# Higher gathered rows of two tiles summed by TensorE through a diagonal of gates, and the last but one block's rows copied ahead of the last weights' rests

## What is computed

```python
gates = jnp.einsum('tk,tke->te', top_w, jax.nn.one_hot(expert_id, N_EXPERTS))
gates = (gates * g_w[:, None]).astype(t.dtype)
for e in range(N_EXPERTS):
    he = jax.nn.silu(t @ w_gate[e]) * (t @ w_up[e])
    y = y + gates[:, e:e + 1] * (he @ w_down[e])
```

## Time and profile before

| | |
|---|---|
| time of 3 runs, us | 1502.73, 1507.63, 1510.17 (median 1507.63) |
| the profiled execution, us | 1509.55, of which the profiled span is 1507.7 |
| busy: PE (TensorE) / DVE (VectorE) / ACT (ScalarE) / POOL (GpSimd) | 95% / 76% / 59% / 40% |
| chain that ended last, by engine | PE 46%, DVE 25%, DMA 15%, issue 7%, ACT 5% |
| DVE sums L375 | 24 (12 a layer), median 1280 ns |
| products L2196 | 32 records (16 a layer), 592 to 1222 ns |

### The profile page before, as it was taken

The page is one execution under the profiler, slowest core; times in us unless marked ns, Lnnn a source line. Parts: engine busy times, 40 slices in busy tenths (PEclk is TensorE's granted clock), DMA queues, the critical chain, the costliest instruction groups (busy, mean ns, idle before and its releaser), DMA issues.

```text
span 1507.7 us, 20546 instructions
## 1 busy us (share of the span) xinstructions
PE 1431.0 (95%) x6830; PEld 1052.0 (70%) x6830; DVE 1152.7 (76%) x1658; ACT 887.7 (59%) x1300; POOL 595.7 (40%) x288
## 2 busy tenths in 40 slices
PE   7999999999999999999799999999989899999995
PEld 4678566567577888877556865665766788887773
DVE  5696887334489999999757958873335899999996
ACT  5733344643558878888485522348345488887880
POOL 2333364060005665554542425521400066655544
PEclk9999999999999999999899999999998899999998
DMA  6333601312149999999651421105041599999995
GB/s 228 95 84 70 222 10 47 140 59 98 70 162 340 399 399 399 398 399 399 216 185 42 112 81 71 57 1 198 1 167 42 183 362 398 398 398 398 398 388 181
DMA packets 151485, 312.75 MB, mean 207 GB/s; under 512 B 33158, under 2 KB 46380, under 8 KB 151228
## 3 DMA queue, kind: packets, MB, share of 16 engines
q1 hardware_dynamic: 140300, 271.39, 49.8%
q0 software_dynamic: 6624, 24.12, 4.3%
q10 hardware_dynamic: 4496, 16.40, 2.7%
HBM read 287.76 MB, written 29.50 MB: 210 GB/s over the span
## 4 chain that ended last, share of the span: by engine, by line
PE 46%; DVE 25%; DMA 15%; issue 7%; ACT 5%; POOL 1%; DVEq 1%; POOLq 0%; SPq 0%; ACTq 0%
PE ps L710 13%; DMA arena<-in_w_down 11%; DVE rest_w_down L1436 8%; PE ps L728 7%; PE ps L1518 4%; DVE rest_w_up L1436 4%; PE ps L1540 3%; DVE rest_w_gate L1436 2%; DVE xg_rest L1449 2%; PE ps L817 2%; PE ps L1636 2%; ACT head_w_down L1431 2%; PE ps L731 2%; DMA arena<-in_w_gate 1%; PE ps L850 1%
## 5 line engine op out<-in xcount | busy, mean ns | idle before, releaser
L2112 POOL TENSOR_TENSOR rest_w_down<-arena,head_w_down 128x2048 fp32r<-128x2048 f32 x30 | 193.4, 6448 | 189.4 <-ACT head_w_down L1431 189.4
L1436 DVE TENSOR_TENSOR rest_w_down<-arena,head_w_down 128x2048 fp32r<-128x2048 f32 x30 | 153.5, 5116 | 12.0 <-ACT head_w_down L1431 11.9
L1436 DVE TENSOR_TENSOR rest_w_gate<-arena,head_w_gate 128x2048 fp32r<-128x2048 f32 x64 | 145.8, 2279 | 0.1
L1436 DVE TENSOR_TENSOR rest_w_up<-arena,head_w_up 128x2048 fp32r<-128x2048 f32 x64 | 143.5, 2281 | 0.1
L1431 ACT ACTIVATE head_w_down<-arena 128x2048 fp32r<-128x2048 f32 x60 | 115.2, 1926 | 39.1 <-DMA arena<-in_w_down 38.9
L1431 ACT ACTIVATE head_w_gate<-arena 128x2048 fp32r<-128x2048 f32 x60 | 114.4, 1919 | 36.1 <-DMA arena<-in_w_gate 35.5
L1431 ACT ACTIVATE head_w_up<-arena 128x2048 fp32r<-128x2048 f32 x64 | 122.0, 1940 | 10.5 <-DMA arena<-in_w_up 10.4
L1420 PE MATMUL ps<-head_w_gate,xg_head 128*128 128x512 f32 x256 | 104.8, 409 | 2.5 <-DVE xg_rest L1449 1.9
L728 PE MATMUL ps<-hT,arena 128*128 128x512 f32 x224 | 104.3, 602 | 2.6 <-ACT arena L951 2.6
L1410 PE MATMUL ps<-head_w_down,he_head 128*128 128x512 f32 x240 | 99.2, 413 | 5.8 <-DVE rest_w_down L1436 2.9
L1422 PE MATMUL ps<-head_w_gate,xg_rest 128*128 128x512 f32 x256 | 101.0, 395 | 0.0
(11 more groups left out here) (381 smaller groups left out, 3519.2 us busy)
## 6 DMA issues: line engine op xcount, KB each, us to landing
arena<-in_w_gate SPq DMA_DIRECT2D x64, 1024.0 KB, 9.9
arena<-in_w_up SPq DMA_DIRECT2D x64, 1024.0 KB, 11.5
arena<-in_w_down SPq DMA_DIRECT2D x64, 1024.0 KB, 10.7
arena<-in_w_in SPq DMA_DIRECT2D x10, 1536.0 KB, 6.7
yrows<-yb ACTq DMA_DIRECT2D x30, 512.0 KB, 6.2
arena<-in_w_in SPq DMA_DIRECT2D x4, 2048.0 KB, 8.7
x<-in_x SPq DMA_DIRECT2D x8, 512.0 KB, 13.9
arena<-in_w_in SPq DMA_DIRECT2D x16, 256.0 KB, 4.9
```

Source lines behind the costliest of these rows:

```text
L1436: nc.vector.tensor_tensor(wl[q][:, c, :], raw[q][:, c, :], wh[q][:, c, :].bitcast(F32), ALU.subtract).then_inc(s_split[q], 1)
L2112: nc.gpsimd.tensor_tensor(wl[2][:, c, :], raw[2][:, c, :], wh[2][:, c, :].bitcast(F32), ALU.subtract)\
```

## The change

It makes six edits. The two scalars of `hot_rows` now hold the gate too, so that LAST comes out of TensorE already multiplied, and its sum is a plain addition of PSUM to x. A new tensor `gate_diag` holds, for tiles 2 and 3, the identity times `early`, made by two instructions on VectorE ahead of `gated(2)`. For tiles 2 and 3 TensorE adds the HIGH rows onto the LAST rows in the same PSUM banks (`high_rows`: a product of `gate_diag` and the gathered rows), and the sums HIGH 2 and HIGH 3 leave VectorE. On TensorE both `row_turned(0)` and `row_turned(1)` now stand behind last_rows 2, high_rows 2, last_rows 3, high_rows 3. VectorE's order between the sums loses the two entries, and `row_inverse(0)` comes after LOW 2. After the loop `outputs` and `h_rest` now stand ahead of both `rest_last`.

```diff
--- before.py
+++ after.py
@@ -300,6 +300,7 @@
         behind = place_of_sel + 4 * (3 * S + KD * LOADED[0])
         hot_rows = nc.alloc_sbuf_tensor_at("hot_rows", [P, NT, P], F32, offset=behind)
         hot = nc.alloc_sbuf_tensor_at("hot", [P, NT, P], F32, offset=behind + 4 * NT * P)
+        gate_diag = nc.alloc_sbuf_tensor_at("gate_diag", [P, NT, P], F32, offset=behind + 8 * NT * P)
 
         up = 3 * SLOT
 
@@ -350,8 +351,8 @@
 
 
         LOW, HIGH, LAST = 0, 1, 2
-        SUMS = [(LOW, 0), (HIGH, 0), (LOW, 1), (HIGH, 1), (LAST, 0), (LOW, 2), (HIGH, 2), (LAST, 1), (LOW, 3), (HIGH, 3), (LAST, 2),
-                (LAST, 3)]
+        SUMS = [(LOW, 0), (HIGH, 0), (LOW, 1), (HIGH, 1), (LAST, 0), (LOW, 2), (LAST, 1), (LOW, 3), (LAST, 2), (LAST, 3)]
+        HIGH_BY_PE = (2, 3)
 
         def summed(l, k, t):
             return len(SUMS) * l + SUMS.index((k, t)) + 1
@@ -365,14 +366,14 @@
             xt = x[:, t, :]
             if k == LAST:
                 dve.wait_ge(sN["hot_out"], t + 1)
-                dve.wait_ge(s_add, summed(l, HIGH, t))
-                rows, g = psw[:, 512 * LAST_BANK(t):512 * LAST_BANK(t) + D], gates[:, t, 1:2]
+                dve.wait_ge(s_add, summed(l, LOW if t in HIGH_BY_PE else HIGH, t))
+                nc.vector.tensor_tensor(xt, xt, psw[:, 512 * LAST_BANK(t):512 * LAST_BANK(t) + D], ALU.add).then_inc(s_add, 1)
             else:
                 dve.wait_ge(s_yg[NT * k + t], 16 * (l + 1))
                 if k == HIGH:
                     dve.wait_ge(s_add, summed(l, LOW, t))
-                rows, g = ya[k][t], early[:, t:t + 1] if k == HIGH else gates[:, t, 0:1]
-            nc.vector.scalar_tensor_tensor(xt, rows, g, xt, ALU.mult, ALU.add).then_inc(s_add, 1)
+                g = early[:, t:t + 1] if k == HIGH else gates[:, t, 0:1]
+                nc.vector.scalar_tensor_tensor(xt, ya[k][t], g, xt, ALU.mult, ALU.add).then_inc(s_add, 1)
 
         xn = view(scratch, 0, 2, D)
 
@@ -2193,7 +2194,17 @@
                     for q in range(2):
                         if t == 0:
                             pe.wait_ge(sN["y_read"], 2 * n + 1 + q)
-                        last = nc.tensor.matmul(ps[LAST_BANK(t) + q], hot[:, t, :], yb[:, 512 * q:512 * q + 512], start=True, stop=True)
+                        last = nc.tensor.matmul(ps[LAST_BANK(t) + q], hot[:, t, :], yb[:, 512 * q:512 * q + 512], start=True,
+                                                stop=t not in HIGH_BY_PE)
+                    if t not in HIGH_BY_PE:
+                        last.then_inc(sN["hot_out"], 1)
+
+                def high_rows(t):
+
+                    pe.wait_ge(s_yg[NT * HIGH + t], 16 * (l + 1))
+                    for q in range(2):
+                        last = nc.tensor.matmul(ps[LAST_BANK(t) + q], gate_diag[:, t, :], ya[HIGH][t][:, 512 * q:512 * q + 512],
+                                                start=False, stop=True)
                     last.then_inc(sN["hot_out"], 1)
 
                 def gate_up(n):
@@ -2224,10 +2235,15 @@
                 last_block = block_count(pe)
                 down_last(last_block)
                 pe.wait_ge(sN["hot_in"], 1)
-                for t in range(NT):
+                pe.wait_ge(sN["hot_one"], 2)
+                last_rows(last_block, 0)
+                last_rows(last_block, 1)
+                for t in HIGH_BY_PE:
                     last_rows(last_block, t)
-                    if l + 1 < L and t >= 2:
-                        row_turned(pe, t - 2)
+                    high_rows(t)
+                if l + 1 < L:
+                    row_turned(pe, 0)
+                    row_turned(pe, 1)
                 if l + 1 < L:
                     idle_products(2)
                     row_turned(pe, 2)
@@ -2368,7 +2384,7 @@
                     do(V.tensor_scalar(R(147, 148), R(141, 142), first_of_last, None, ALU.subtract))
                     do(V.scalar_tensor_tensor(early.unsqueeze(2), R(147, 148), 0.0, gates[:, :, 1:2], ALU.is_lt, ALU.mult))
                     for t in range(NT):
-                        do(V.tensor_scalar(hot_rows[:, t, :], iota, rout[:, t, 147:148], None, ALU.is_equal),
+                        do(V.tensor_scalar(hot_rows[:, t, :], iota, rout[:, t, 147:148], gates[:, t, 1:2], ALU.is_equal, ALU.mult),
                            "hot_one" if t == NT - 1 else None, wait=False)
 
                 weights_rest(dve, 1, 1, 1)
@@ -2377,6 +2393,10 @@
                 before_gated(2)
                 h_rest(1)
                 weights_rest(dve, 2, 1, 1)
+                do = engine(dve, cm_)
+                for t in HIGH_BY_PE:
+                    do(nc.vector.tensor_scalar(gate_diag[:, t, :], ident, early[:, t:t + 1], None, ALU.mult),
+                       "hot_one" if t == NT - 1 else None, wait=False)
                 gated(2)
                 with dve.Fori(1, last_two_out(dve)) as k:
                     before_gated(k + 2)
@@ -2384,7 +2404,7 @@
                     h_rest(k + 1)
                     weights_rest(dve, 2, 1, k + 1)
                     gated(k + 2)
-                last = block_count(dve)
+                last, second_last = block_count(dve), last_two_out(dve)
 
                 def scaled(do, t):
                     row_inverse(dve, do, t)
@@ -2396,24 +2416,23 @@
                     nc.vector.tensor_tensor(last_rest[:, c, :], last_raw[:, c, :], last_head[:, c, :].bitcast(F32), ALU.subtract)\
                       .then_inc(s_split[2], 1)
 
+                outputs(second_last)
+                h_rest(last)
                 dve.wait_ge(s_head[2], 2 * last + 1)
                 rest_last(2)
-                outputs(last_two_out(dve))
-                h_rest(last)
                 rest_last(3)
                 if l + 1 == L:
                     for k, t in SUMS:
                         add_rows(dve, l, k, t)
                 else:
                     do = engine(dve, cv_)
-                    for k, t in SUMS[:7]:
+                    for k, t in SUMS[:6]:
                         add_rows(dve, l, k, t)
                     row_inverse(dve, do, 0, "rows_inv")
                     add_rows(dve, l, LAST, 1)
                     add_rows(dve, l, LOW, 3)
                     row_out(dve, do, l + 1, 0, 0, "rows_hT")
                     row_inverse(dve, do, 1, "rows_inv")
-                    add_rows(dve, l, HIGH, 3)
                     add_rows(dve, l, LAST, 2)
                     row_out(dve, do, l + 1, 1, 0, "rows_hT")
                     add_rows(dve, l, LAST, 3)
```

## The result

| | before | after |
|---|---|---|
| median, us | 1507.63 | 1511.31 |
| ratio, 95% interval | | 1.0025 [1.0015, 1.0035] |
| profiled execution, us (span) | 1509.55 (1507.7) | 1509.51 (1507.7) |

The change makes the kernel slower by 3.8 us (2.3 to 5.3), which is within half a per cent and yet clear of noise over this many runs (19 of each; one of each took over twice the usual time, 4994 and 3979 us, and is left out of the ratio). Forecast were +3.4 and 1511.0. The two profiled executions happen to have the same span: that of after is one of its quicker ones, that of before one of its slower ones. So their totals say nothing of the change; the stretches inside them do, counted from one event that both have.

A forecast was written before the change was run, and what follows sets the result against it. It took the chains of waits at both layers' ends as the bound, not TensorE's 95% busy share. Terms +3.85 (layer 0) - 0.93 (layer 1) + 0.5 (experts' start) = +3.4 us, from 1507.63 to 1511.0; range 1504.2 to 1516.3.

The forecast's parts named there:

- The hand-over in layer 0: Layer 0's end: row_turned(0) waits behind sixteen TensorE records, partly at half clock, making hT_head 3.85 us late.
- so nothing gives this back: Behind hT_head: ScalarE, VectorE, then TensorE chain without gaps, so the full 3.85 us delay stays.
- The early copy: Behind the expert loop, both layers: VectorE's half of y 0.93 us earlier, store 0.92, gathers and LAST 0 by 0.93.
- so no: Store of the last but one block's y does not wait for ScalarE's he_head; if it did, the gain would be 0.49.
- The cover: Moved rests cost nothing: rest_last(2) takes 1.21 us, not 5.02, and down_last needs it only after six products, 1.4 us.
- Layer 1: Layer 1's end: sixteen TensorE records take 8.57 us, LAST 3 alone remains, ending 1503.6 against 1504.51; gain 0.93.
- The experts' start: VectorE there: hot_rows adds 0.25 us a layer, 0.5 for both; gate_diag taken as nothing, as loads set the pace.
- (a): Rival: TensorE does not fall to half clock, sixteen records take 6.9 us; sum +0.5, 1508.1 us; chance 0.07.
- (b): Rival: layer 0's hand-over swallows its delay because a load or the store of x is last; 1506.3 us; chance 0.12.
- (c): Rival: clock stays at half through all sixteen records; sum +13.7, 1521.3 us; chance 0.05.
- (d): Rival: experts' start not absorbed and the store held by he_head; +6.2, 1513.8 us; chance 0.16.
- (e): Rival: gathers do not start earlier, their pace being the DMA's, not the store's; +0.93 each, 1512.9 us; chance 0.05.

The follow-up runs named there:

- pe_only: Changed kernel with the early copy undone (rest_last(2) ahead of outputs again); 1511.75 us, ratio to before 1.0036.
- store_reg: Changed kernel with the last but one block's number loaded once on ScalarE, ahead of its half of y; 1511.60 us, ratio to before 1.0029.
- front_more: Changed kernel with twelve more gate_diag-like instructions on VectorE ahead of gated(2) in both layers; 1525.40 us, ratio to before 1.0129.
- diag_late: Changed kernel with the two gate_diag instructions moved behind the loop; 1511.92 us, ratio to before 1.0029.
- front_only: Kernel before with only the added experts'-start work (two-scalar hot_rows, two unread gate_diag instructions, LAST as plain sum); 1507.66 us, ratio 1.0004.
- copy_only: Kernel before with only outputs and h_rest moved ahead of both rest_last; 1505.98 us, ratio 0.9996.
- layer1_only: Changed kernel with HIGH 2 and 3 through TensorE in layer 1 alone, layer 0's sums and turns as before; 1508.00 us, ratio to before 1.0007.
- clock_kept: Changed kernel with five idle products of ones on TensorE ahead of tile 2's last_rows; 1506.59 us, ratio to before 1.0003.
- turn_late: Kernel before with only layer 0's row_turned(0) and row_turned(1) moved behind tile 3's last_rows; 1506.73 us, ratio 1.0002.

## Why the prediction was right, step by step

**The hand-over in layer 0: right up to hT_head, wrong behind it.** Forecast: row_turned(0) behind sixteen records that take 9.42 us, LAST 3 4.0 later, hT_head 3.85 later. Measured: 749.10 to 758.38 is 9.28; y0 to the end of LAST 3 went from 29.08 to 33.09; hT_head 3.9 later against y0. Over the executions: with the changed order, products and half clock (after, pe_only, store_reg, front_more, diag_late), and 0.64 added where the store was early (0.82 in store_reg), y0 to hT_head is 39.4 on average, 38.8 to 39.7; with the old order and all sums on VectorE (before, front_only, copy_only, layer1_only) 34.9, 34.4 to 35.5. Difference 4.4, less 0.64 is 3.8. The clock came back after 4.7 us, where 5.14 had been taken. clock_kept puts 2.5 of it on the half clock, turn_late 1.7 on the order; the two can't simply be added. The step that failed is "so nothing gives this back": behind hT_head some 1.9 us came back on average (421.2 against 423.0 to layer 1's first gather), and 3.65 in the two profiled executions. The term to the time is then some +1.9 and not +3.85.

**The early copy: right in kind, too large by 0.28 us.** VectorE's half came 0.84 earlier, as forecast (0.93), but the store only 0.64. The answer "so no" (the store doesn't wait for he_head) was right, as store_reg shows. The step that failed is the 0.19 from the end of VectorE's half to the issue, taken from inside the loop: it was 0.37. What I had missed is the load of a register that stands between them behind the loop only; store_reg shows 0.18 of it. The rest is that VectorE's half starts 0.07 behind ScalarE's, where the forecast had it 0.02 ahead. The cover was as described: rests at 2.35 for two, and down_last not late.

**Layer 1: wrong in sign.** Forecast -0.93; the two profiled executions have -1.2, but they mislead. The step that failed is taking the end of before from one execution, in which HIGH 3 came 1.48 late, and setting TensorE's queue (10.1 us from restart to the end of LAST 3) equal to it. TensorE's queue measured 10.0 in after, and 9.8 to 11.2, on average 10.5, over the seven kernels that have it at half clock; VectorE's seven sums need 8.5 to 8.7 when they need not wait. From y0 to the end of LAST 3, corrected for the early store in the same way, the kernels with high_rows at half clock have 28.3 on average of seven (27.1 to 29.6), those with all sums on VectorE and without added products 26.7 of four (26.0 to 27.8). That is +1.6 for TensorE's part, -0.64 for the copy: +1.0 and not -0.93. With such a spread the +1.0 is good to some 1 us; that TensorE's part costs is shown by the 9.8 against 8.7.

**The experts' start: right in size, its reason half wrong.** 0.5 was taken, 0.6 (at most 2) measured by front_only. hot_rows: 0.87 became 1.11 for four, as forecast. That a delay is absorbed because the DMA engines are full is not contradicted for 0.4 us (diag_late), and fails for 3.84, after which their share falls to 0.39.

**The sum.** +3.8 (to hT_head), -1.9 (given back behind it), +1.0 (layer 1's end) and +0.6 (experts' start) make 3.5, against 3.8 (2.3 to 5.3) of the times; each term is good to no better than some 1 us. The forecast's 3.4 owes its nearness to luck: the end of layer 1 was too low by 1.9, and taking nothing for what comes back behind hT_head was too high by 1.9.

**The rivals.** (a) No fall of the clock: the granted clock was 0.50 until about 753.8, as before, so no. (b) The hand-over swallowed by the store of x: no, hT_head followed ScalarE's last step into hT by 0.08 and waited for no store. But about half of the delay was made good behind hT_head, by another way than the rival names. (c) Half clock throughout: no; it came back 4.7 and 3.3 us after the restart in after. Over all runs it took up to 6.1, beyond the 5.14 that the forecast's bounds rest on. (d) The bounds together: no, as front_only has at most 2 us and the store was not held by he_head (store_reg). (e) The gathers did start earlier, with the store (4.58 after y0, 5.22 before).

## What to carry to other kernels

An operation that is taken off a busy engine onto an idle one also moves the queue of that engine: ask what stands behind it there, and at which clock an engine starts that has been idle. Compare the new route with what the old one takes when nothing is late, from several executions, not with the one in the profile. Follow a delay beyond the end of its stretch before adding it to the time: here some 1.9 of 3.8 us came back in the layer behind. Filling an idle stretch of TensorE with products that nobody reads is worth a try where many float32 products follow at once: it gave 2.5 us in the changed kernel's hand-over, and less than could be seen in the old one, where VectorE and a store came last.

## What the runs showed that I had not expected

A load of a register on ScalarE between an operation and a DMA issue held the issue by 0.18 us. The same four gathers and five sums, from the first gather to tile 2's last_rows, took 11.7 to 13.8 us from one execution to the next. The store of tile 3 of x took 5.84 to 7.53 us where hT_head waited for it. Two TENSOR_SCALAR of 128x128 with one input in SBUF took 4.21 us and not 0.47 beside a GpSimd operation. By the Trainium skill (SBUF — State Buffer, Who interferes with whom) a VectorE instruction in a two-port mode, which a tensor_scalar can enter, and a GpSimd instruction exclude one another, and whichever issues first has the ports for the whole of it. The row agrees: the GpSimd operation had begun 2.72 earlier, and the two ended 0.28 after it. A delay of 3.84 us of VectorE at the start of a loop whose loads it releases cost 8 us a layer in the time, 6.5 and 5.6 of them in the experts' stretch. And TensorE's clock fell a second time some 16 us behind hT_head in four of the thirteen traces, for 1.4 us, in kernels whose work there is the same.
